# Four-tap convolution on GpSimd, eleven selection rounds before the recurrence, and a new order of recurrence and attention

## Chip, core and metric

One NeuronCore of a Trainium2 chip runs the whole program in one launch. The metric is the device time of that launch in microseconds (us). The core has five engines with queues of their own: TensorE (PE in the profile, PEld its weight loads), VectorE (DVE), ScalarE (ACT), GpSimd (POOL) and SyncE (SP), which here only issues DMAs. An engine works through its queue in order and waits on counting semaphores.

## What is computed

The reference is one inference step of a small decoder: 512 prompt tokens and 8 sequences with 4 new tokens each (32 sample tokens, 544 columns in all), two layers, width 1024, float32. A layer multiplies its input by one wide matrix, and the columns go to four branches of width 256:

```python
y_a = attn(q, k, v, qi, ki, wi)            # a token indexer scores all keys; only the top 128 (129) count
y_b, rwkv_state, shift_buf = rwkv7_mix(cols[..., B_START:B_END], ...)   # linear recurrence, 64x64 states
y_c, convc_buf = gated_short_conv(cols[..., C_START:C_END], ...)        # three-tap convolution, gated
y_d, convd_buf, lru_h = rglru_block(cols[..., D_START:D_END], ...)      # four-tap convolution, gated recurrence
mix = concatenate([y_a, y_b, y_c, y_d]) @ w_out                         # then layer norm, 16 experts, layer norm
```

The four-tap convolution of branch D adds to `w[0]*x[t-3]` the products of three more taps and a bias, per channel. Its result feeds two sigmoid gates (matrix products) and the input of that branch's recurrence. The selection of branch A needs, per query, a threshold below the largest 128 (prompt) or 129 (sample) scores.

## The kernel before

All matrices are float32 and every layer is written as five queue programs that run side by side: `sync_program`, `pool_program`, `tensor_program`, `scalar_program` and `vector_program`. The order inside each queue is written out by hand. Semaphores count events per layer (`nth(l, name, n)`). Inside the recurrence, three lists of names (`RW_PE`, `RW_DVE`, `RW_ACT`, lines 175 to 182) say which count on `rw_mm`, `rw_v` and `rw_a` stands for which result, so the lists must follow the order in the queues.

A layer goes through these stages.

*Projections.* `columns` of TensorE computes 17 chunks of 128 channels by 544 tokens (line 755), ScalarE copies each from PSUM to a ring of four buffers `fm` (line 1391), and the small products of the branches stand between the chunks: indexer, LoRA, key norms, bonuses, and after chunk 11 the gate products `lru_gates` (lines 815 and 816, by `product`). Chunks 0 to 6 belong to the recurrence, 7 and 9 to the four-tap convolution, 8 and 10 to its output gate, 11 to 16 to the three-tap convolution in two halves.

*VectorE during the projections* (`columns` of `vector_program`): it mixes the chunks, computes decays (`decays`), key rates (`key_rates`, `bonus`), both halves of the four-tap convolution (`conv_d`, lines 1952 to 1965, by `taps`, lines 1892 and 1895), normalised keys (`key_norms`, lines 1940 to 1948: clamp, reciprocal of 1152 columns, products), the inputs of the recurrence (`chunk_inputs`, lines 2053 to 2059) and branch D (`lru_decay`, `lru_input`, `lru`, lines 1969 to 2000). In between it runs ten rounds of the selection. A round finds the eight largest values of each of four score tiles (512, 384, 256 and 544 columns; line 2300) and replaces them by a very small number (line 2307).

*GpSimd during the projections* (`pool_program`): row stores, then `conv_c` for both halves (lines 588 to 616), each when its three chunks are there. ScalarE may copy chunks 15 and 16 only when `conv_c` is through with the first half's buffers (`fc_used`).

*Recurrence* (`rwkv`): the prompt is cut into 8 blocks of 64 tokens. TensorE forms many 64x64 products (`diagonal`, line 893), VectorE masks and adds from PSUM (lines 2073, 2104, 2148, 2164), ScalarE copies (line 1391). At the start TensorE computes `bar0 ab0 bar1 ab1 kar0`, after a wait for all 17 chunk copies; VectorE's masks follow in `first(0)`, `first(1)`, `keys(0)`. In between VectorE runs selection rounds 10 to 15 in quarters (`selection_quarter`, lines 2317 and 2319): 24 quarters, six of them in the last part. That last part passes the state through the blocks: `step(c)` on TensorE, `state(c)` on VectorE, by turns. Beside it run the sample tokens: products with their old states (`s_m0`, `s_m1`), two masked reductions (lines 2183 and 2187), `spread` (lines 2194 to 2197), three products for each half of the new states (`s_t0`, `s_t1`) and their scaling (line 2210). `finish_selection` (round 16, then the additive masks `bias`, lines 2325 to 2330) stands before that scaling. The end of the recurrence, `rw_v` at its last count, lets SyncE load key pages (line 484) and GpSimd value pages (line 651).

*Attention* (`prompt_attention`, `sample_logits`, `sample_attention`): for each of four blocks of 128 queries logits (line 1120), masking and row maxima on VectorE (`masked`, lines 2352 to 2359), exponentials on ScalarE (`exps`, line 1637), scaling (`normed`, line 2367), transposes and products with the values (`output(i)`, lines 1139 and 1128). Before, all of `masked(0..2)` precede `normed(0..2)`; TensorE does `output(0)`, `logits(3)`, `output(1)`, both halves of the sample logits (line 1177), `output(2)`, `output(3)`. Norms of branch B stand between (`y_sums`, line 1099).

Then come the output projection, the norm, the router and the experts, which the diff leaves alone.

## Time and profile before

| | us |
|---|---|
| median of three runs | 1319.84 |
| lowest and highest | 1317.95, 1325.25 |
| the profiled execution's own time | 1318.73 |
| span of its trace | 1317.1 |
| mean granted clock of TensorE over the span | 0.927 of full |

The profile shows one execution. Its page lists busy time per engine, the chain of work that ended last (each piece led back to what released it) and groups of instructions by source line. A line such as 893 belongs to a helper that many products share, so times within a stage are read from the timeline (instructions in order of time) and from windows (busy time of each engine in a stretch). A float32 matrix product shows as two instructions. Idle time before an instruction stands in brackets, with the engine whose work ended it.

### The profile page before, as it was taken

Reading aid. Unit: us, or ns where it says so; the run is one execution under the profiler, and the core shown is the slowest. Engines: PE = TensorE matmul, PEld = TensorE weight load, DVE = VectorE, ACT = ScalarE, POOL = GpSimd, SP = SyncE. Lnnn points to the kernel's source line nnn. Section 1 sums busy time; section 2 is a strip of 40 time slices with the busy share of each in tenths; the row PEclk is TensorE's granted clock in tenths of the full one; section 3 lists DMA queues with packets and bytes.
Section 4 is the critical chain, followed back from the end, with each engine's and each line's share of the span. In section 5 each row is a group of like instructions: output and inputs, shape, how many; then the busy total and the mean of one; then the engine's idle time right before and its main releaser. Section 6 shows DMA issues by size and latency. Waiting matters only on the chain.

```text
span 1317.1 us, 24577 instructions
## 1 busy us (share of the span) xinstructions
PE 1127.5 (86%) x9786; PEld 685.4 (52%) x9786; DVE 651.4 (49%) x1353; ACT 327.9 (25%) x774; POOL 165.4 (13%) x225
## 2 busy tenths in 40 slices
PE   8999998987899369999599999999778982999940
PEld 4587777973545323332256777889434451333310
DVE  0046898875633611111643588988772453111128
ACT  0234341303421111111244343412053210111100
POOL 0130008105000020000301000450230002000020
PEclk9989999998999679999799999999889985999975
DMA  7199110007660769997522112100296247699742
GB/s 285 56 395 354 48 56 26 7 3 225 208 260 1 319 233 354 423 423 257 203 77 65 57 48 64 33 21 4 64 275 256 101 168 300 245 410 421 300 150 103
DMA packets 66548, 240.37 MB, mean 183 GB/s; under 512 B 8738, under 2 KB 28354, under 8 KB 57026
## 3 DMA queue, kind: packets, MB, share of 16 engines
q1 hardware_dynamic: 46800, 169.15, 33.9%
q0 software_dynamic: 14592, 52.10, 10.9%
q10 hardware_dynamic: 5042, 17.54, 3.3%
q8 instruction: 79, 1.29, 0.4%
q14 instruction: 35, 0.29, 0.1%
HBM read 190.21 MB, written 50.78 MB: 183 GB/s over the span
## 4 chain that ended last, share of the span: by engine, by line
PE 82%; DVE 5%; issue 3%; ACT 3%; DMA 2%; SPq 2%; DVEq 2%; POOL 1%; POOLq 0%; ACTq 0%
PE ps L755 20%; PE ps L1299 13%; PE ps L893 11%; PE ps L1256 8%; PE ps L1314 7%; PE ps L701 4%; PE ps L735 4%; SPq L484 2%; PE ps L815 2%; PE ps L1286 2%; PE ps L1128 1%; PE ps L711 1%; ACT arena L1391 1%; PE ps L1235 1%; PE ps L1223 1%
## 5 line engine op out<-in xcount | busy, mean ns | idle before, releaser
L1391 ACT ACTIVATE arena<-ps 128x512 f32<-128x512 f32 (+14 forms) x342 | 142.3, 454 | 612.4 <-PE ps L755 137.3
L755 PE MATMUL ps<-arena 128*128 128x272 f32 x1088 | 259.7, 397 | 0.0
L755 PEld LDWEIGHTS ps<-arena 128*128 128x128 f32 x1088 | 206.4, 192 | 47.8 <-issue 4.0
L1299 PE MATMUL ps<-arena 128*32 128x512 f32 x1536 | 169.7, 592 | 4.8 <-ACT arena L1391 4.8
L893 PE MATMUL ps<-arena 64*64 64x64 f32 (+3 forms) x4016 | 150.6, 234 | 18.8 <-DVE arena L2164 12.1
L893 PEld LDWEIGHTS ps<-arena 64*64 64x64 f32 x4016 | 137.3, 136 | 31.2 <-issue 18.0
L1256 PE MATMUL ps<-arena 128*128 128x512 f32 x256 | 112.4, 594 | 0.0
L1299 PEld LDWEIGHTS ps<-arena 128*32 128x32 f32 x1536 | 51.3, 110 | 116.9 <-issue 116.9
L1314 PE MATMUL ps<-arena 128*32 128x512 f32 x768 | 87.4, 595 | 3.3 <-DVE arena L2623 2.0
L2617 DVE COPY arena<-ps 128x256 f32<-128x256 f32 x24 | 10.2, 425 | 140.2 <-PE ps L1331 140.2
L1256 PEld LDWEIGHTS ps<-arena 128*128 128x128 f32 x256 | 47.5, 189 | 56.5 <-issue 56.5
L711 PE MATMUL ps<-arena 128*128 128x512 f32 x34 | 23.2, 852 | 49.2 <-DMA rows_in<-arena,ints 37.0
L2623 DVE COPY arena<-ps 128x512 f32<-128x512 f32 x24 | 16.6, 693 | 91.0 <-PE ps L1314 91.0
L701 PE MATMUL ps<-arena 128*128 128x420 f32 (+1 forms) x128 | 52.3, 571 | 5.1 <-DMA arena<-in_xT 5.1
L735 PE MATMUL ps<-arena 128*128 128x512 f32 (+1 forms) x128 | 52.7, 569 | 3.1 <-ACT arena L1696 3.1
L1696 ACT ACTIVATE arena<-ps,arena 128x128 f32<-128x128 f32 (+1 forms) x112 | 38.8, 451 | 58.4 <-PE ps L1223 43.4
L1314 PEld LDWEIGHTS ps<-arena 128*32 128x32 f32 x768 | 23.2, 109 | 50.1 <-issue 47.7
L2307 DVE MATCH_REPLACE8 arena<-arena 32x544 f32<-32x544 f32 (+3 forms) x82 | 47.1, 585 | 0.0
L2300 DVE MAX8 arena<-arena 32x8 f32<-32x544 f32 (+3 forms) x82 | 43.7, 589 | 1.7
L1725 ACT ACTIVATE arena<-ps 128x256 f32<-128x256 f32 x24 | 9.3, 386 | 137.6 <-PE ps L1299 137.6
L701 PEld LDWEIGHTS ps<-arena 128*128 128x128 f32 x128 | 24.9, 196 | 31.8 <-issue 26.7
L711 PEld LDWEIGHTS ps<-arena 128*128 128x128 f32 x34 | 9.2, 281 | 61.9 <-DMA rows_in<-arena,ints 37.3
(348 smaller groups left out, 1333.2 us busy)
## 6 DMA issues: line engine op xcount, KB each, us to landing
arena<-in_w_gu SPq DMA_DIRECT2D x32, 2048.0 KB, 13.8
arena<-in_w_dn SPq DMA_DIRECT2D x32, 1024.0 KB, 14.4
arena<-in_wf SPq DMA_DIRECT2D x34, 512.0 KB, 3.7
rows_in<-arena POOLq DMA_DIRECT2D x12, 1024.0 KB, 25.1
arena<-rows_in SPq DMA_DIRECT2D x24, 512.0 KB, 13.8
rows_out<-arena ACTq DMA_DIRECT2D x24, 512.0 KB, 8.6
arena<-in_cache_v POOLq DMA_DIRECT2D x64, 128.0 KB, 5.7
arena<-in_cache_k SPq DMA_DIRECT2D x64, 128.0 KB, 5.5
```

Of the source, the lines that this page charges most:

```text
L701: mm = pe.matmul(ps[:, k, 0:w], m.xT[:, c, row_tile(k % NT)], m.wa[:, c, a:a + w], start=c == 0, stop=c == KC - 1, skip_group_check=True)
L711: pe.matmul(ps[:, 7, :], ident, m.consts[:, 0:512], start=True, stop=True)
L735: mm = pe.matmul(ps[:, k % 2, 0:w], m.xT[:, c, row_tile(i)], m.wa[:, c, a:a + w], start=c == 0, stop=c == KC - 1)
L755: mm = pe.matmul(ps[:, 2 + 2 * h + n % 2, 0:HALF], m.wf[n % 3][:, c, :], m.xT[:, c, h * HALF:h * HALF + HALF], start=c == 0, stop=c == KC - 1)
L893: mm = pe.matmul(out[q], lhsT[q], rhs[q], start=start, stop=stop, skip_group_check=check)
L1256: mm = pe.matmul(ps[:, 2 * (i % 2) + h, :], m.yT[:, c, row_tile(i)], m.wout[c // 4][:, c % 4, 512 * h:512 * h + 512], start=c == 0, stop=c ...
L1299: mm = pe.matmul(ps[q, 3 + k, :], m.xgT[:, c, q], m.w_gu[HOME[i]][:, c, :], start=c == 0, stop=c == KC - 1, skip_group_check=True)
L1314: mm = pe.matmul(ps[q, 5 + h, :], m.hT[:, f, q], m.w_dn[HOME[i]][:, f, 512 * h:512 * h + 512], start=f == 0, stop=f == 1, skip_group_check ...
L1391: return act.activation(out, in_, ACT.Copy)
L1696: ins = act.activation(m.xT[:, c, P * i:P * i + n], ps[:, 4 + c // 4, n * (c % 4):n * (c % 4) + n], ACT.Identity, bias=m.lnc[:, 1, c:c + 1 ...
L2300: dve.max(m.top8[c][rows], m.score[c][rows])
L2307: dve.match_replace(m.score[c][rows], m.top8[c][rows], m.score[c][rows], TAKEN)
```

## The change

- `conv_d` moves from VectorE's program to GpSimd's, ahead of `conv_c`. There a tap is a multiplication into a scratch tile and an addition, with drains between. It waits for its chunk and for the indexer's last tiles (`relu_done`, `rl_used`), whose memory its output takes. ScalarE's copies of chunks 11 to 14 now wait for `conv_done`, which GpSimd raises after each half, in place of VectorE's `fm_used`.
- VectorE runs one selection round more before `lru`, so the recurrence holds rounds 11 to 15: 20 quarters, two of them in the last part.
- The recurrence starts with `bar0 kar0`, and the wait for the last chunk copies stands behind them. VectorE's masks follow that order. In its last part the sample tokens' products are spread between the steps, and `finish_selection` leaves it.
- `finish_selection` now follows `masked(0)` in attention. `logits(3)` precedes `output(0)`, `masked(3)` precedes `normed(2)`, and the two halves of the sample logits stand before and behind `output(2)`, on ScalarE as on TensorE.
- The key pages lie in memory as (sequence, page, half, key), so a page's two halves are adjacent for each partition: pieces of 1024 bytes instead of 512. The sample logits read them with a stride.

The core of the diff:

```diff
-RW_PE = counts("bar0 ab0 bar1 ab1 kar0 d2_0 d2t_0 d2_1 d2t_1 kar1 d4_0 d4t_0 d4_1 d4t_1 tb0 tb1 d8_0 d8_1 tv0 tv1 "
+RW_PE = counts("bar0 kar0 ab0 bar1 ab1 d2_0 d2t_0 d2_1 d2t_1 kar1 d4_0 d4t_0 d4_1 d4t_1 tb0 tb1 d8_0 d8_1 tv0 tv1 "
                "x4_0 x4_1 ta0 ta1 x2_0 x2_1 tk0 tk1 x1_0 x1_1 wv0 wv1 xt_0 xt_1 s_bar ft_0 ft_1 s_t s_kar "
-               "z1_0 z1_1 s_d2 z2_0 z2_1 s_z s_wv z3_0 z3_1 s_pp pp0 pp1 gx0 gx1 h0 y0 h1 y1 "
-               "h_1 s_rc h_2 h_3 s_m0 s_m1 h_4 h_5 h_6 s_y h_7 y_7 s_t0 s_t1")
-RW_DVE = counts("q0 dt0 q1 dt1 km0 d2_0 d2_1 km1 d4_0 d4_1 x8_0 x8_1 x4_0 x4_1 x2_0 x2_1 x1_0 x1_1 s_q s_km z1_0 z1_1 s_x "
-                "z2_0 z2_1 s_z z3_0 z3_1 s_pp pp0 pp1 gx0 gx1 t1 t2 s_rc t3 t4 t5 s_w t6 s_u0 t7 s_u1 t8 s_t0 s_t1")
+               "z1_0 z1_1 s_d2 z2_0 z2_1 s_z s_wv z3_0 z3_1 s_pp pp0 pp1 gx0 gx1 h0 y0 s_rc h1 s_m0 s_m1 y1 "
+               "h_1 h_2 h_3 s_y h_4 h_5 s_t0 h_6 s_t1 h_7 y_7")
+RW_DVE = counts("q0 km0 dt0 q1 dt1 d2_0 d2_1 km1 d4_0 d4_1 x8_0 x8_1 x4_0 x4_1 x2_0 x2_1 x1_0 x1_1 s_q s_km z1_0 z1_1 s_x "
+                "z2_0 z2_1 s_z z3_0 z3_1 s_pp pp0 pp1 gx0 gx1 t1 s_rc s_w t2 t3 t4 t5 s_u0 t6 s_u1 t7 s_t0 t8 s_t1")
...
-    m.K = [view(at, 2, 4, PAST) for at in (R2, XT0)]
+    m.K = [view(at, 4, NPAGE, 2, PAGE) for at in (R2, XT0)]
...
-            sp.dma_start(m.K[g][:, :, j:j + 1, PAGE * c:PAGE * c + PAGE],
-                         din["cache_k"][bass.ds(l * NPHYS + page, 1)].rearrange("z p q k -> p q z k"))\
+            sp.dma_start(m.K[g][:, j, c:c + 1, :, :],
+                         din["cache_k"][bass.ds(l * NPHYS + page, 1)].rearrange("z p q k -> p z q k"))\
...
-    def taps(out, tmp, src, w):
+    def taps(out, tmp, src, w, bias=None):
 
         width = SEQ if len(src.shape) == 2 else DS
+        first = 4 - len(w)
 
         def at(k):
-            return src[:, 1 + k:1 + k + width] if len(src.shape) == 2 else src[:, :, 1 + k:1 + k + width]
-
-        pool.tensor_scalar(out, at(0), w[0], None, mul)
-        for k in range(1, 3):
+            return src[:, first + k:first + k + width] if len(src.shape) == 2 else src[:, :, first + k:first + k + width]
+
+        pool.tensor_scalar(out, at(0), w[0], bias, mul, add) if bias is not None else pool.tensor_scalar(out, at(0), w[0], None, mul)
+        for k in range(1, len(w)):
             pool.tensor_scalar(tmp, at(k), w[k], None, mul)
             pool.drain()
             pool.tensor_tensor(out, out, tmp, add)
             pool.drain()
+
+    def conv_d(l, j):
+        convd = m.param("convd").rearrange("p (j b t) -> p j b t", j=2, b=DB)
+        tail = m.small("convd").rearrange("p (j c) -> p j c", j=2)
+        dw, db = m.param("dw"), m.param("db")
+        n = 7 + 2 * j
+        xb = n % 4
+        pool.wait_ge(s["fm_copied"], nth(l, "fm_copied", n + 1))
+        pool.wait_ge(s["relu_done"], nth(l, "relu_done", 12))
+        pool.wait_ge(s["rl_used"], nth(l, "rl_used", 12))
+        pool.tensor_tensor(m.turn, m.const("ones"), m.const("ones"), ALU.add)
+        pool.drain()
+        pool.tensor_copy(m.fm_s[xb][:, :, 0:3], convd[:, j, :, :])
+        pool.drain()
+        w = [dw[:, 4 * j + k:4 * j + k + 1] for k in range(4)]
+        taps(m.xc[:, j, 0:SEQ], m.tap[:, 0:SEQ], m.fm_p[xb], w, db[:, j:j + 1])
+        taps(seqs(m.xc[:, j, SEQ:T]), seqs(m.tap[:, SEQ:T]), m.fm_s[xb], w, db[:, j:j + 1])
+        pool.tensor_copy(tail[:, j, 0:3], m.fm_p[xb][:, SEQ:3 + SEQ])
+        pool.tensor_copy(tail[:, j, 3:27].rearrange("p (b t) -> p b t", t=3), m.fm_s[xb][:, :, 4:7])
+        pool.drain().then_inc(s["conv_done"], 1)
 
...
+        conv_d(l, 0)
+        conv_d(l, 1)
...
-        pe.wait_ge(s["fm_copied"], nth(l, "fm_copied", NCH))
         pe.wait_ge(s["job_out"], nth(l, "job_out", 12))
-        for g in range(2):
-            wide(2 * g, lambda k: cut(m.BE, g, k), lambda k: both(g, k)).then_inc(s["rw_mm"], 1)
+        def barred(g):
+            return wide(2 * g, lambda k: cut(m.BE, g, k), lambda k: both(g, k))
+
+        def turned_bar(g):
             for k in range(8):
                 mm = diagonal(ps[:, 4 + g, CH * k:CH * k + CH], cut(AE, g, k), cut(m.BE, g, k))
-            mm.then_inc(s["rw_mm"], 1)
+            return mm
+
+        barred(0).then_inc(s["rw_mm"], 1)
         wide(6, lambda k: cut(m.KE, 0, k), lambda k: both(0, k)).then_inc(s["rw_mm"], 1)
+        pe.wait_ge(s["fm_copied"], nth(l, "fm_copied", NCH))
+        turned_bar(0).then_inc(s["rw_mm"], 1)
+        barred(1).then_inc(s["rw_mm"], 1)
+        turned_bar(1).then_inc(s["rw_mm"], 1)
...
+        grown(0).then_inc(s["rw_mm"], 1)
+        read(0).then_inc(s["rw_mm"], 1)
+        v("gx0")
+        for p in range(2):
+            mm = diagonal(ps[:, 4, NS * p:NS * p + NS], m.sPP[:, p, 1, :], m.sQ[:, p, 1, 0:NS])
+        mm.then_inc(s["rw_mm"], 1)
+        grown(1).then_inc(s["rw_mm"], 1)
+        v("gx1")
+        v("s_rc")
+        pe.wait_ge(s["state_in"], nth(l, "state_in", 32))
+        for p in range(2):
+            diagonal(ps[:, 5 + p, :], m.sLR[:, p, :], m.TB[:, p]).then_inc(s["rw_mm"], 1)
+        read(1).then_inc(s["rw_mm"], 1)
+        step(1)
+        step(2)
+        step(3)
+        v("s_w")
+        sample_rows_out().then_inc(s["rw_mm"], 1)
+        step(4)
+        step(5)
+        v("s_u0")
+        sample_state(0).then_inc(s["rw_mm"], 1)
+        step(6)
+        v("s_u1")
+        sample_state(1).then_inc(s["rw_mm"], 1)
+        step(7).then_inc(s["rw_mm"], 1)
 
...
         logits(2)
+        logits(3)
         pe.wait_ge(s["yn_std"], nth(l, "yn_std", 1))
         output(0)
-        logits(3)
         output(1)
-        sample_logits(l)
+        sample_logits(l, 0)
         output(2)
+        sample_logits(l, 1)
         output(3)
 
-    def sample_logits(l):
...
+            elif n >= 11:
+                act.wait_ge(s["conv_done"], nth(l, "conv_done", 1 if n < 13 else 2))
...
-        for g in range(2):
-            act.wait_ge(s["s_lg_mm"], nth(l, "s_lg_mm", g + 1))
-            copy(m.s_lg[g][:, 0:PAST], ps[:, 2 - 2 * g, :])
-            copy(m.s_lg[g][:, PAST:T], ps[:, 3 - 2 * g, 0:NS]).then_inc(s["s_lg"], 1)
+        sample_logits(0)
         turned(2)
         output(2)
+        sample_logits(1)
...
-        conv_d(l, 0)
         block_queries(l)
         select_rounds(1)
-        conv_d(l, 1)
...
-        select_rounds(1)
+        select_rounds(2)
...
-        quarters = iter(range(4 * 10, 4 * 16))
+        quarters = iter(range(4 * 11, 4 * 16))
...
-        first(0)
-        first(1)
+        near(0)
         keys(0)
+        turned(0)
+        near(1)
+        turned(1)
...
         mm("h0")
         state(0)
-        select(4)
-        mm("h_1")
-        state(1)
+        select(1)
         mm("s_rc")
         tt(m.sLR[:, :, NS:2 * NS], ps[:, 4, 0:2 * NS].rearrange("p (k n) -> p k n", n=NS), m.AR[:, 1, :, SEQ:T], add)\
             .then_inc(s["rw_v"], 1)
-        mm("h_2")
-        state(2)
-        mm("h_3")
-        state(3)
-        mm("h_4")
-        state(4)
+        select(1)
         for p in range(2):
             mm(f"s_m{p}")
             tt(m.sM[p], ps[:, 5 + p, :].rearrange("p (b n) -> p b n", n=CH),
...
-        mm("h_5")
-        state(5)
+        for c in range(1, 4):
+            mm(f"h_{c}")
+            state(c)
 
         def spread(p):
             own = m.const("s_rows").unsqueeze(2).broadcast_to([P, DB, CH])
-            tt(m.sW[:, p, :], m.sW[:, p, :], m.sPP[:, p, 0, :], add)
-            dve.drain()
             tt(m.UEb[p], m.sW[:, p, :].unsqueeze(1).broadcast_to([P, DB, CH]), own, mul)
             tt(m.VEb[p], m.sT[:, 2, p, :].unsqueeze(1).broadcast_to([P, DB, CH]), own, mul).then_inc(s["rw_v"], 1)
 
-        select(2)
-        mm("s_y")
-        spread(0)
-        mm("h_6")
-        state(6)
-        spread(1)
-        mm("h_7")
-        state(7)
-        finish_selection()
-        for p in range(2):
+        def sample_out(p):
             mm(f"s_t{p}")
             tt(m.TB[:, p], ps[:, 4 + p, :].rearrange("p (b n) -> p b n", n=CH),
                m.ec_s[:, p].unsqueeze(2).broadcast_to([P, DB, CH]), mul).then_inc(s["rw_v"], 1)
+
+        mm("s_y")
+        tt(m.sW, m.sW, m.sPP[:, :, 0, :], add)
+        mm("h_4")
+        state(4)
+        dve.drain()
+        spread(0)
+        mm("h_5")
+        state(5)
+        spread(1)
+        mm("h_6")
+        state(6)
+        sample_out(0)
+        mm("h_7")
+        state(7)
+        sample_out(1)
+        dve.drain()
 
     def y_centred(l):
         dve.wait_ge(s["fc_used"], nth(l, "fc_used", 2))
...
         y_centred(l)
-        for i in range(3):
-            masked(i)
-        for i in range(3):
-            normed(i)
+        masked(0)
+        finish_selection()
+        masked(1)
+        masked(2)
+        normed(0)
+        normed(1)
         masked(3)
+        normed(2)
...
```

The bodies that are only moved are left out: VectorE's old `conv_d`, the old order of the recurrence's end on TensorE (`grown` and `read` for both groups first, then the steps, then both sample state products) and `sample_logits`, which now takes the half `g` as an argument.

## Rows read from the trace of the kernel before

**Rows 1.** The page's first part: busy us, share, instructions of TensorE.

```profile
PE 1127.5 (86%) x9786; PEld 685.4 (52%) x9786; DVE 651.4 (49%) x1353; ACT 327.9 (25%) x774; POOL 165.4 (13%) x225
```

**Rows 2.** Chain of waits, 170 to 232 us: start, length, what.

```profile
217.47 3.55 issue
```

**Rows 3.** Timeline: end of the projections, first masks in both layers.

```profile
219.52 1.40 ACT L1391 ACTIVATE arena<-ps 128x272 f32<-128x272 f32 x6 [10.10 <-POOL arena L616]
...
224.65 6.56 DVE L2073 TENSOR_TENSOR arena<-ps,arena 128x512 f32<-128x512 f32 x12 [3.67 <-PE ps L893]
...
866.24 6.56 DVE L2073 TENSOR_TENSOR arena<-ps,arena 128x512 f32<-128x512 f32 x12 [2.14 <-PE ps L893]
```

**Rows 4.** Windows: us; PE, PEld, DVE, ACT, POOL busy; clock; DMA share; GB/s.

```profile
181.00:217.50 36.50, 36.47 (x159) 29.70 (x157) 34.81 (x82) 12.37 (x21) 16.94 (x17) 1.00 0.10 30
...
262.00:284.60 22.60, 22.44 (x653) 22.25 (x648) 17.00 (x41) 1.48 (x3) 0.00 (x0) 1.00 0.01 4
288.30:291.20 2.90, 0.01 (x2) 0.00 (x0) 2.70 (x4) 0.00 (x0) 0.00 (x0) 1.00 0.00 0
292.70:299.00 6.30, 3.60 (x24) 1.74 (x26) 5.90 (x16) 0.78 (x2) 0.00 (x0) 0.50 0.01 1
326.00:330.00 4.00, 4.00 (x11) 1.47 (x10) 0.47 (x1) 0.19 (x1) 0.00 (x0) 0.50 1.13 311
```

**Rows 5.** Chain of waits, 270 to 334 us: recurrence's end, attention.

```profile
291.29 2.36 DVE arena L2319 x5
...
295.40 7.73 PE ps L893 x40
...
325.77 3.71 PE ps L1120 x8
```

**Rows 6.** Timeline of TensorE in layer 1: second half of the sample logits.

```profile
979.24 0.18 PEld L1177 LDWEIGHTS ps<-arena 128*32 128x32 f32 x8 [0.20 <-DMA arena<-in_cache_k]
```

**Rows 7.** Timeline, 136 to 182 us: chunk 7, key norms, gate products, chunk inputs.

```profile
136.48 0.75 ACT L1391 ACTIVATE arena<-ps 128x272 f32<-128x272 f32 x3 [6.67 <-PE ps L755]
...
158.12 1.32 ACT L1525 ACTIVATE arena<-ps 128x512 f32<-128x512 f32 x4
...
161.14 0.76 DVE L1940 TENSOR_SCALAR arena<-arena 128x1152 f32<-128x1152 f32 x1
...
174.93 1.02 PE L815 MATMUL ps<-arena 128*128 128x512 f32 x2
...
177.46 1.36 DVE L2057 TENSOR_TENSOR arena<-arena 128x1152 f32<-128x1152 f32 x1
```

**Rows 8.** GpSimd's groups by shape: count, busy us, mean ns, idle before.

```profile
L592 POOL TENSOR_TENSOR arena<-arena 128x512 f32<-128x512 f32 x8 | 10.2, 1272 | 1.2 <-issue 0.2
...
L588 POOL TENSOR_SCALAR arena<-arena 128x512 f32<-128x512 f32 x4 | 6.3, 1567 | 0.7 <-issue 0.7
```

**Rows 9.** Timeline, 182 to 216 us: GpSimd's first convolution beside VectorE.

```profile
184.08 2.09 DVE L2300 MAX8 arena<-arena 128x8 f32<-128x512 f32 x4
...
198.65 0.19 POOL L604 COPY arena<-arena 128x16 f32<-128x16 f32 x1 [2.23 <-issue]
...
207.29 3.53 POOL L590 TENSOR_SCALAR arena<-arena 128x512 f32<-128x512 f32 x1 [0.17 <-issue]
208.19 1.28 DVE L1978 SCALAR_TENSOR_TENSOR arena<-arena 128x1088 f32<-128x1088 f32 x1
...
213.26 0.25 POOL L592 TENSOR_TENSOR arena<-arena 128x32 f32<-128x32 f32 x1
...
214.20 1.35 POOL L592 TENSOR_TENSOR arena<-arena 128x32 f32<-128x32 f32 x1
```

**Rows 10.** Timeline of VectorE, 262 to 304 us: state 0, end of the selection.

```profile
277.58 0.29 DVE L2164 TENSOR_TENSOR arena<-ps,arena 128x128 f32<-128x128 f32 x1 [0.45 <-PE ps L893]
...
296.97 0.70 DVE L2300 MAX8 arena<-arena 32x8 f32<-32x544 f32 x1
...
300.68 0.17 DVE L2330 TENSOR_TENSOR arena<-arena 32x32 f32<-32x32 f32 x1
```

More of the change, by code:

```diff
@@ new lines, in sample_logits @@
+        pe.wait_ge((s["k0_in"], s["k1_in"])[g], nth(l, f"k{g}_in", 256))
+        a = 2 - 2 * g
+        pe.wait_ge(s["qb_ready"], nth(l, "qb_ready", 1))
+        pe.wait_ge(s["lg_taken"], nth(l, "lg_taken", 4))
+        for j in range(4):
+            for p in range(2):
+                pe.matmul(ps[32 * j:32 * j + 32, a, :].rearrange("m (c k) -> m c k", c=NPAGE), m.QB[:, p, 4 * g + j, :], m.K[g][:, j, :, p, :],
+                          start=p == 0, stop=False, skip_group_check=True)
+        pe.matmul(ps[:, a, :], spread[0:NS, P * g:P * g + P], bias[0:NS, 0:PAST], start=False, stop=True,
+                  skip_group_check=True)
@@ L2083, in select, with near @@
                 selection_quarter(*divmod(next(quarters), 4))
-        def first(g):
+        def near(g):
             mm(f"bar{g}")
@@ L2091, in first, with turned @@
             ins.then_inc(s["rw_v"], 1)
+        def turned(g):
             mm(f"ab{g}")
```

71 lines of the change are left out of this document (21 added, 50 removed).

## The prediction

> **What bounds the kernel now.** First the page: TensorE is busy 86% of the span [rows 1], so a gain has to shorten a stretch in which TensorE waits or runs slowly. The change touches three such stretches of each of the two layers: the end of the projections, the recurrence's last third, and attention. Experts, output projection and norms keep their code and are taken to move along unchanged.
>
> *End of the projections.* The chain of waits shows TensorE standing still 3.55 us between the last projection and the recurrence [rows 2]. The timeline tells why: ScalarE copies the last two chunks only after GpSimd's first convolution, a wait of 10.10 us [rows 3]. VectorE has little to spare there: it is busy 34.81 of 36.5 us [rows 4] and idles 3.67 us (layer 0) and 2.14 us (layer 1) before the recurrence's first mask, from 220.98 and 864.10 on [rows 3]. Who is late next when TensorE stops waiting is therefore VectorE.
>
> *Recurrence.* From 262 to 284.6 TensorE is busy 22.44 of 22.6 us [rows 4]; nothing that VectorE gives back there counts. Behind 284.6 it waits for VectorE twice: 2.9 us without work (288.3 to 291.2), then 2.7 idle us before the sample products at 295.40; these run partly at a granted clock of 0.50, 1.2 GHz [rows 4, 5].
>
> *Attention.* The fourth block's logits lie on the chain, 3.71 us, at a clock of 0.50 [rows 4, 5]. Key loads matter once: in layer 1 the second half of the sample logits starts 0.20 us after a key page lands [rows 6].
>
> **The change, part by part** (us per layer).
>
> *Convolution on GpSimd.* VectorE loses both conv_d, but gains little of their length. key_norms starts at 161.14 because conv_d(1) precedes it; without that it waits for ScalarE's square root, which ends at 159.44 [rows 7]. So 1.7 us come free; conv_d(0)'s share falls into an earlier wait for ScalarE's head copies.
>
> GpSimd needs per conv_d four multiplications (1.57) and three additions (1.27) of 512 columns [rows 8], the same seven of 32 columns (some 0.3 each; a free addition takes 0.25 [rows 9]), small copies and gaps of some 0.15: 6.3 + 3.8 + 2.2 + 2.7 = 15. The first multiplication also adds a bias, which no row shows; I take 1.57, with 3.53, the longest multiplication seen [rows 9], as the upper end; below the one-operation row there is no reason to go. The first instruction after a long pause is followed by a 2.23 us gap [rows 9]. Chunk 7 is copied at 137.2 [rows 7]: the first convolution ends at 137.2 + 2.2 + 15 + some 3.5 of blocking (next paragraph) = 158, the second would end at 173, ahead of the gate products at 174.93 [rows 7].
>
> But the two engines exclude each other. GpSimd's multiplication of 207.29 took 3.53 us, because VectorE's two-input operations ran until 209.47; a 32-column addition took 1.35 instead of 0.25 beside another one [rows 9]. After the reciprocal key_norms and chunk_inputs are seven two-input operations of some 1.35 (they end at 177.46 + 1.36 [rows 7]). They meet GpSimd's last addition and its seven small operations, so both take turns. I place GpSimd's end at 182 and VectorE's delay at c = 3.0 (bounds 0, never meeting, and 6, four full GpSimd operations in their way). TensorE waits in the second gate product from 176.1 to 182: 5.9 us. A pause of that length can halve the clock, as before the sample products [rows 4], some 1.6 us more.
>
> In row 207.29 GpSimd lost the turn to an operation (208.19) that asked later. The Trainium skill ("SBUF — State Buffer", Who interferes with whom) says that whoever issues first gets the port pair for the whole instruction. By that rule GpSimd would get every second turn, and c would be 3.6 instead of 3.0, 1.2 us more in all; row 207.29 contradicts it, so I keep 3.0. The same section has VectorE's one-input tensor_scalar block GpSimd too; no row here shows it, and by it key_norms' first operation would wait up to one GpSimd operation more.
>
> *Eleventh round.* Four maxima (2.09 [rows 9]) and four replacements (2.36 [rows 5]) with their gaps: 4.6 us, on VectorE's tight stretch. VectorE reaches the masks at 220.98 - 1.7 + 4.6 + 3.0 = 226.9 in layer 0, at 864.10 + 5.9 = 870.0 in layer 1.
>
> *Recurrence entry.* TensorE now starts bar0 and kar0 before waiting for the last chunk copies, so the 3.55 us wait is covered by those two groups. With the gate stall it starts at 217.5 + 5.9 = 223.4; its first result is used 2.1 us later (VectorE's idle time in layer 1 [rows 3]), 225.5, or 227 with the 3.6 of layer 0 (221.02 to 224.65 [rows 2, 3]). VectorE's 226.9 decides. Against 224.65 and 866.24 [rows 3] the masks start 2.3 and 3.8 later. **Entry: +6.1 in both layers together**, bounds 0 (c = 0) and +12 (c = 6).
>
> VectorE's key masks now precede the DT mask, which puts TensorE's first wait 1.3 us later behind the masks' start; slack of TensorE covers that (five groups of products lie before it), and if not it costs 1.3.
>
> *Recurrence tail.* Four quarter rounds, the final round and the bias building leave it. State 0 is at 277.58 [rows 10]; the same three groups of products follow, 2 us each, now with 1.9 us of sample products between them: step 1 at 285.3. VectorE's two reductions hold state 1 to 286.1. Three states at 0.85 a turn and the sample rows: 288.7. State 4 and the first spread (two operations of 0.69): 290.7. Sample state products 2.6 (six passes of 0.43), step 6, the second 2.6, step 7 and two VectorE operations: 297.7, where it was 303.85. **-6 per layer, -12.** Seen from the other side: the two waits (2.9 + 2.7) and 2.1 of half clock go [rows 4], 1.7 of new turns come. If the clock falls again it is -4; at best -6.5.
>
> *Attention.* The final selection round and the biases, 296.97 to 300.85, 3.9 us [rows 10], were hidden by the sample products of 295.40 (7.73 us [rows 5]). Now they stand between masked(0) and masked(1): masked(2) ends 4.8 later, the third exponentials 1.6 later, and with them ScalarE's first turned copy. But logits(3) fills that pause, and its 3.71 leave the way to output(1), which thus starts 2.1 earlier. Splitting the sample logits around output(2) keeps their sum; the exponentials behind the second half take back 0.9. With output(0) no longer at clock 0.50, 0.5 more: **-1.7 per layer, -3.4** (bounds +1.6, nothing filled, and -2.5).
>
> *Key pages.* SP's queue issues as many loads in the same order, each with half the packets. In layer 1 the last lands at 979.2, 33.6 us after the recurrence; the second half of the sample logits will ask at 36.8. Margin 3.2: no cost, no gain. GpSimd's queue has the value loads behind its convolutions as before, far behind. conv_c waits behind conv_d, but its inputs come at 196, after 182. ScalarE's copies of chunks 11 to 14 wait for conv_d instead of VectorE; chunk 13 leaves TensorE after the gate stall anyway.
>
> **Sum.** +6.1 - 12 - 3.4 = -9.3 against the profiled execution, 1318.73 (span 1317.1): 1309.4. The median is 1.1 above it, so 1310.
>
> **Rivals.**
> *GpSimd is on time* (0.2): the operations hardly meet, c is 0, conv_d(1) ends before 176, entry 0. For it: maxima, replacements and the reciprocal do not meet GpSimd's work in any row. Then -15.4: 1304.
> *The gain stays off the path* (0.18): the clock falls in the tail (-8), attention gives 3.2 instead of taking, entry +6: about +1, 1321. For it: VectorE works 5.90 of 6.3 us in the tail and TensorE still idles between its turns [rows 4].
> *GpSimd comes too late* (0.12, slower): conv_d(1) holds TensorE in the gate products. If every operation of conv_d is blocked (3.53 for a multiplication, 1.27 + 1.3 for an addition, 1.35 for a small one [rows 9]), each convolution takes 34 us and the second ends at 207; TensorE stalls 31, starts at 248.5, and the masks come 26 late in each layer: +52 - 15.4 = +37, 1355. It makes the kernel slower by over 0.5% once the entry costs 22 in all, which is a second convolution that ends after 192. Against it: the mean addition and first multiplication are at their unblocked length [rows 8].
>
> **How the numbers follow.** The forecast itself has 0.5, range 1302 to 1316: entry bounds against tail -8. No change means within 0.5% (6.6 us, about what a measurement of this kernel can tell): 1313.2 to 1326.4. Faster: 0.42 of the forecast's 0.5 plus 0.2 = 0.62; same: 0.08 + 0.18 = 0.26; slower 0.12. The range takes in all but the late GpSimd and some edges: 1300 to 1326.
>
> **What would show it.** Right: GpSimd's second four-tap convolution ends near 182 and TensorE waits some 6 us between the first and second gate product; masks start near 227 at VectorE's hand; no wait over 1 us for VectorE among the recurrence's last products; fourth logits before the first transposes. Wrong: a gate stall over 16 us, masks that start before 224, a tail longer than 24 us behind state 0, or second sample logits waiting for pages.

## The result and the profile after

| | before | after |
|---|---|---|
| median, us (6 runs each, same chip) | 1324.31 | 1311.57 |
| lowest and highest | 1317.95, 1325.25 | 1308.91, 1316.64 |
| profiled execution's own time | 1318.73 | 1311.37 |
| span of its trace | 1317.1 | 1309.7 |

The ratio is 0.9916, with a 95% interval of 0.9888 to 0.9945: the changed kernel is faster by 0.8%, and the 1310 that was predicted is 1.6 us off. As a change it is 2.9 off: the medians fell by 12.7, and the forecast was 9.8 below the 1319.84 that it started from. One execution of what follows, of run 10's kernel, took 2053 us at a granted clock of 0.55 and is left out of its times.

The table below gives the stages of the two traces, counted from the start of TensorE's first gate product (174.93 and 818.42 before, 174.17 and 813.48 after). All later comparisons use these columns, because the clock of the stages ahead differs from run to run.

| us | first mask | state 0 | attention starts | output projection | last part (state 0 to attention) | attention |
|---|---|---|---|---|---|---|
| before, layer 0 | 49.72 | 102.65 | 129.07 | 189.08 | 26.42 | 60.01 |
| before, layer 1 | 47.82 | 100.76 | 127.23 | 187.42 | 26.47 | 60.19 |
| after, layer 0 | 49.75 | 102.76 | 123.04 | 181.98 | 20.28 | 58.94 |
| after, layer 1 | 49.41 | 101.73 | 122.02 | 182.92 | 20.29 | 60.90 |

Up to state 0 the change costs 0.11 and 0.97 us, the recurrence's last part gives 6.14 and 6.18, attention gives 1.07 and takes 0.71: 11.6 us in all. The two profiled executions differ by 7.4 only; the other 4.2 lie outside these stages (0.8 won ahead of layer 0's first gate product, 2.9 lost between the layers, 2.0 lost behind layer 1's attention). Part of that is the clock: one group of layer 1's projections took 9.32 us at a granted clock of 0.82, where it took 7.64 at 1.00 before.

**Gate products** (where [rows 7] had 174.93 for the first). TensorE's timeline after, layer 0 and then layer 1, in which line 838 is the gate product:

```profile
174.17 1.02 PE L838 MATMUL ps<-arena 128*128 128x512 f32 x2
...
178.35 2.08 PE L838 MATMUL ps<-arena 128*128 128x512 f32 x2 [3.01 <-POOLq L614]
...
180.51 2.05 PE L838 MATMUL ps<-arena 128*128 128x512 f32 x2
...
817.76 1.12 PE L838 MATMUL ps<-arena 128*128 128x512 f32 x2 [3.12 <-POOLq L614]
```

Line 614 raises `conv_done`: the second convolution is 3 us late in both layers. The windows of layer 0 show what follows (columns as in [rows 4]; the one before the DMA share is the granted clock):

```profile
174.00:178.00 4.00, 1.34 (x6) 0.70 (x4) 3.81 (x7) 2.90 (x6) 3.40 (x5) 1.00 0.40 131
178.00:182.00 4.00, 3.65 (x6) 1.94 (x7) 3.85 (x12) 0.87 (x2) 0.25 (x2) 0.50 0.00 0
185.00:189.00 4.00, 4.00 (x18) 3.27 (x18) 3.85 (x11) 1.96 (x3) 0.00 (x0) 1.00 0.00 0
```

Behind the wait the products run at 0.50 (1.2 GHz) and take 2.08 instead of 1.02 us. In layer 1 a wait of 3.12 us is followed by the full clock (1.12).

**GpSimd beside VectorE** ([rows 8, 9] before). Four lines of GpSimd's timeline in layer 0, three of VectorE's at the same moments, then one of GpSimd's and one of VectorE's from layer 1:

```profile
139.39 1.11 POOL L589 TENSOR_SCALAR arena<-arena 128x512 f32<-128x512 f32 x1 [0.21 <-issue]
...
156.84 0.76 POOL L589 TENSOR_SCALAR arena<-arena 128x512 f32<-128x512 f32 x1 [0.18 <-issue]
...
168.85 2.58 POOL L591 TENSOR_SCALAR arena<-arena 128x32 f32<-128x32 f32 x1
...
177.02 0.37 POOL L591 TENSOR_SCALAR arena<-arena 128x32 f32<-128x32 f32 x1 [0.17 <-issue]
...
158.72 1.04 DVE L1982 TENSOR_SCALAR arena<-arena 128x1152 f32<-128x1152 f32 x1 [2.88 <-ACT arena L1564]
...
168.71 1.37 DVE L1988 SCALAR_TENSOR_TENSOR arena<-arena 128x1152 f32<-128x1152 f32 x1
170.00 1.28 DVE L1990 TENSOR_TENSOR arena<-arena 128x1088 f32<-128x1088 f32 x1
...
843.63 1.49 POOL L593 TENSOR_TENSOR arena<-arena 128x512 f32<-128x512 f32 x1
843.91 2.37 DVE L2005 SCALAR_TENSOR_TENSOR arena<-arena 128x1088 f32<-128x1088 f32 x1
```

GpSimd's multiplication of 32 columns takes 2.58 us beside VectorE's two-input operations and 0.37 free of them. VectorE's seven operations of `key_norms` and `chunk_inputs` keep their 1.28 to 1.41 us in layer 0: in this stretch GpSimd alone pays. Elsewhere VectorE pays too: the last line, an operation of branch D, takes 2.37 us behind an addition of 512 columns that GpSimd started just ahead of it, and the same operation takes 1.28 in layer 0, where GpSimd was busy with a multiplication. The first operation of `key_norms` starts 15.45 us ahead of the first gate product, where it was 13.79.

**Entry** (against the masks of [rows 3] and state 0 of [rows 10]). VectorE's timeline, layer 0 and layer 1:

```profile
223.92 3.74 DVE L2098 TENSOR_TENSOR arena<-ps,arena 128x512 f32<-128x512 f32 x7 [2.28 <-PE ps L916]
...
276.93 0.29 DVE L2193 TENSOR_TENSOR arena<-ps,arena 128x128 f32<-128x128 f32 x1 [0.45 <-PE ps L916]
...
862.89 6.20 DVE L2098 TENSOR_TENSOR arena<-ps,arena 128x512 f32<-128x512 f32 x12 [0.26 <-PE ps L916]
```

In layer 0 VectorE idles 2.28 us before its first mask, so TensorE decides; in layer 1 it idles 0.26, no more than where it waits for nothing (run 1 below), so VectorE decides.

**Last part of the recurrence** (against the waits and the 7.73 us of [rows 4, 5]). TensorE's timeline after:

```profile
285.82 0.68 PE L916 MATMUL ps<-arena 64*64 64x64 f32 x16 [0.92 <-DVE arena L2193]
286.66 1.85 PE L916 MATMUL ps<-arena 64*64 64x64 f32 x56 [0.16 <-DVE arena L2193]
288.67 0.68 PE L916 MATMUL ps<-arena 64*64 64x64 f32 x16 [0.16 <-DVE arena L2193]
290.06 6.30 PE L916 MATMUL ps<-arena 64*64 64x512 f32 x56 [0.71 <-DVE arena L2218]
297.21 1.10 PE L1136 MATMUL ps<-arena 128*128 128x512 f32 x2 [0.85 <-DVE arena L2222]
```

```profile
290.00:297.20 7.20, 6.30 (x56) 2.70 (x57) 3.19 (x8) 0.60 (x1) 0.00 (x0) 1.00 0.01 2
```

No wait is over 0.92 us (0.93 in layer 1), and the sample products run without a pause and at the full clock, where [rows 4] have 0.50.

**Attention** (against line 1120 in [rows 5]). TensorE's timeline, then a window with the columns as above:

```profile
309.10 1.56 PE L1157 MATMUL ps<-arena 64*128 64x384 f32 x8 [2.45 <-DVE arena L2381]
312.52 1.99 PE L1157 MATMUL ps<-arena 64*128 64x512 f32 x8 [1.86 <-DVE arena L2385]
...
317.07 0.43 PE L1165 MATMUL ps<-arena 128*64 128x128 f32 x2 [1.34 <-ACT arena L1428]
```

```profile
320.00:324.00 4.00, 3.95 (x16) 2.33 (x14) 3.93 (x4) 1.25 (x4) 0.00 (x0) 0.50 1.07 343
```

The fourth block's logits (second line) now run at the full clock, but wait 1.86 us for the third masking, which reads the same PSUM banks. Behind that run of waits the half clock has moved on to the second half of `output(0)` and to `output(1)`.

### The profile page after: what moved, and what is told of

It is laid out like the page before. It is cut to its first block, busy times and chain, and to the rows that moved or that the text cites. A ratio compares the mean times of both kernels' runs of the same rounds, so it can differ in the third digit from the quotient of the medians.

```text
span 1309.7 us, 24635 instructions
## 1 busy us (share of the span) xinstructions
PE 1129.9 (86%) x9786; PEld 686.6 (52%) x9786; DVE 638.1 (49%) x1307; ACT 328.4 (25%) x774; POOL 224.3 (17%) x297
## 4 chain that ended last, share of the span: by engine, by line
PE 73%; DVE 7%; issue 6%; POOLq 4%; ACT 3%; DMA 2%; POOL 2%; DVEq 2%; ACTq 0%; SPq 0%
PE ps L778 13%; PE ps L1336 13%; PE ps L916 10%; PE ps L1293 9%; PE ps L1351 7%; PE ps L724 4%; PE ps L758 4%; POOLq L592 2%; PE ps L1165 2%; POOLq L594 2%; PE ps L1323 2%; ACT arena L1428 1%; PE ps L734 1%; POOL arena L591 1%; POOL rows_in L684 1%
## 5 line engine op out<-in xcount | busy, mean ns | idle before, releaser
L778 PEld LDWEIGHTS ps<-arena 128*128 128x128 f32 x1088 | 206.5, 191 | 48.2 <-issue 4.0
L916 PE MATMUL ps<-arena 64*64 64x64 f32 (+3 forms) x4016 | 145.6, 231 | 5.5 <-DVE arena L2193 2.5
L916 PEld LDWEIGHTS ps<-arena 64*64 64x64 f32 x4016 | 134.6, 134 | 16.8 <-issue 10.0
L1293 PEld LDWEIGHTS ps<-arena 128*128 128x128 f32 x256 | 48.1, 191 | 57.7 <-issue 57.6
L591 POOL TENSOR_SCALAR arena<-arena 128x512 f32<-128x512 f32 (+1 forms) x40 | 50.9, 1273 | 4.1 <-issue 4.1
L2336 DVE MATCH_REPLACE8 arena<-arena 32x544 f32<-32x544 f32 (+3 forms) x90 | 51.6, 585 | 0.0
L2329 DVE MAX8 arena<-arena 32x8 f32<-32x544 f32 (+3 forms) x90 | 47.9, 589 | 1.9
```

Source lines behind the costliest of these rows:

```text
L591: pool.tensor_scalar(tmp, at(k), w[k], None, mul)
L778: mm = pe.matmul(ps[:, 2 + 2 * h + n % 2, 0:HALF], m.wf[n % 3][:, c, :], m.xT[:, c, h * HALF:h * HALF + HALF], start=c == 0, stop=c == KC - 1)
L916: mm = pe.matmul(out[q], lhsT[q], rhs[q], start=start, stop=stop, skip_group_check=check)
L1293: mm = pe.matmul(ps[:, 2 * (i % 2) + h, :], m.yT[:, c, row_tile(i)], m.wout[c // 4][:, c % 4, 512 * h:512 * h + 512], start=c == 0, stop=c ...
L2329: dve.max(m.top8[c][rows], m.score[c][rows])
L2336: dve.match_replace(m.score[c][rows], m.top8[c][rows], m.score[c][rows], TAKEN)
```

## The experiments

Ten runs. The diffs are against the changed kernel, except where noted, and leave out lines that only follow from those shown (counts, indices, moved bodies, the matching order on ScalarE). The times are counted from the first gate product again, and each ratio is to the kernel before on the same chip.

**1. The convolution back on VectorE, all else as changed.**

```diff
@@ pool_program
-        conv_d(l, 0)
-        conv_d(l, 1)
         conv_c(l, 0)
@@ vector_program, columns
+        conv_d(l, 0)
         block_queries(l)
         select_rounds(1)
+        conv_d(l, 1)
         key_norms(l)
```

> The changed kernel with one part undone: the four-tap convolution is back on VectorE, eleven rounds and all new orders stay. Times are counted from the start of TensorE's first gate product; in the changed kernel the first mask of the recurrence comes at 49.75 (layer 0) and 49.41 (layer 1), the last projections start at 10.77 and 7.84. Theory A (the move frees VectorE by 1.7 us only, and costs TensorE a gate stall): the last projections start at 5.6 in both layers again; VectorE reaches the masks 1.7 to 2 later than now, so they come at 49.4 to 50 in layer 0 and at 51 in layer 1, and the whole kernel stays within 3 us of the changed one, ratio to the kernel before 0.990 to 0.995. Theory B (the move is what pays for the eleventh round): VectorE gets back the 4.3 and 5.6 us that the two convolutions took on it, the masks come 8 to 10 later in each layer, and the ratio is 1.004 or more.

Ratio 0.9966 (0.9937 to 0.9995), between the two theories: some 6 us slower than the changed kernel, with intervals that touch. The last projections start at 5.44 again (10.60 and 7.67 in the changed kernel), and the masks come at 51.62 and 51.40, by 1.9 and 2.0 later. State 0 comes 3.3 and 3.9 later (106.10 and 105.66). Timeline of layer 0 (the mask, then TensorE's wait for it), then a window:

```profile
225.33 6.20 DVE L2111 TENSOR_TENSOR arena<-ps,arena 128x512 f32<-128x512 f32 x12 [0.26 <-issue]
...
229.13 11.07 PE L914 MATMUL ps<-arena 64*64 64x64 f32 x250 [5.62 <-DVE arena L2111]
```

```profile
230.00:234.00 4.00, 4.00 (x82) 4.00 (x80) 3.28 (x7) 0.60 (x1) 2.87 (x8) 0.50 0.02 4
```

TensorE stands still 5.62 us and then runs at 0.50. The masks are near theory A in layer 1 (it gave 51), and later than its 49.4 to 50 in layer 0: VectorE is ready for them 3.9 us later than in the changed kernel (51.36 against 47.47), and 2.0 later in layer 1. Only 1.3 and 1.2 of that lie ahead of branch D. Most of the other 2.6 and 0.8 lies in it, where GpSimd's three-tap convolution now runs beside VectorE's two-input operations (one of 1088 columns takes 2.37 us in both layers). The half clock behind a late VectorE (1.5 us in layer 0, 1.9 in layer 1) was in neither theory.

**2. Ten rounds; four quarters more in the last part.**

```diff
@@ vector_program, columns
-        select_rounds(2)
+        select_rounds(1)
         lru(l)
@@ vector_program, rwkv
         state(0)
-        select(1)
+        select(4)
         mm("s_rc")
...
-        select(1)
+        select(2)
```

> The changed kernel with ten selection rounds before the recurrence instead of eleven; the four quarters that this leaves over go back into the recurrence's last part (four behind state 0, two behind the sample rows). In the changed kernel that part, from state 0 to the first product of attention, takes 20.3 us in both layers. Theory A (VectorE's selection work made the last part long): it grows by 3 us per layer (four quarters are 4.6, some 1.6 of idle time is there to take them); the masks stay where they are in layer 0, where VectorE idles 2.28 before them, and come 2.6 earlier in layer 1; in sum +3 to +4, ratio 0.993 to 0.995. Theory B (the new order of the last part made it short, the quarters fit into VectorE's idle time there): the last part grows by 1 us at most, and layer 1's earlier masks make the kernel 1 to 2 us faster than the changed one, ratio 0.990.

Ratio 0.9939 (0.9902 to 0.9976). The last part took 22.56 and 23.77 us, 2.3 and 3.5 more; the masks came at 49.81 and 46.84. Theory A to the letter, so at these places quarters cost. Whether it was they that made the last part of before long is the next question's.

**3. The kernel before, VectorE relieved, old order kept** (diff against the kernel before).

```diff
@@ vector_program, columns
-        select_rounds(1)
+        select_rounds(2)
         lru(l)
@@ vector_program, rwkv
         state(0)
-        select(4)
+        select(1)
...
-        select(2)
+        select(1)
         mm("s_y")
...
-        finish_selection()
@@ vector_program, attention
         masked(0)
+        finish_selection()
         masked(1)
```

> The kernel before with only VectorE's selection work moved: eleven rounds before the recurrence, one quarter in place of four behind state 0, one in place of two behind state 5, the end of the selection in attention between the first and the second masking. The order of the products in the recurrence's last part, the convolution on VectorE, the entry and the key layout are those of before. The last part took 26.4 us before and takes 20.3 in the changed kernel. Theory A (the selection work made it long): 21.5 or less. Theory B (the order of the sample products made it long): 23.5 or more. In between both have a share. The entry is later than before by up to 4.6 us (the eleventh round) less the 3.67 and 2.14 that VectorE idled there.

The last part took 26.91 and 26.19 us: nothing won (1330.16 us in a single run). Timeline of layer 0, then a window:

```profile
283.12 0.29 DVE L2164 TENSOR_TENSOR arena<-ps,arena 128x128 f32<-128x128 f32 x1 [4.17 <-PE ps L893]
...
290.95 2.35 PE L893 MATMUL ps<-arena 64*64 64x64 f32 x40 [2.93 <-DVE arena L2164]
...
295.19 8.12 PE L893 MATMUL ps<-arena 64*64 64x64 f32 x40 [1.90 <-DVE arena L2164]
```

```profile
293.00:297.00 4.00, 2.10 (x28) 1.35 (x26) 3.35 (x8) 0.82 (x2) 0.00 (x0) 0.50 0.01 2
```

VectorE idles 4.17 us at the start, and TensorE's wait of 2.93 (two reductions stand between states 3 and 4) is there as in [rows 4]. The wait before the sample products is 1.90 instead of 2.78 us, but the half clock takes that back: here it sets in earlier (the products of 290.95 take 2.35 us, and 1.38 in the kernel before). With the order of before, less selection makes the part no shorter: theory B.

**4. The end of the selection in VectorE's two waits of the last part.**

```diff
@@ vector_program, rwkv
+        selection_round(16)
         mm("h_6")
         state(6)
         sample_out(0)
+        biases()
         mm("h_7")
@@ vector_program, attention
         masked(0)
-        finish_selection()
```

> The changed kernel with the end of the selection back in the recurrence, but cut in two: the last round (1.7 us) stands before state 6, the additive masks (2.1 us) before state 7, where VectorE waits 1.73 and 2.15 us for TensorE. Theory A (in attention the end of the selection stands on the chain: TensorE waits 2.45 to 2.73 us for the second masking and 1.86 for the third): the last part of the recurrence stays at 20.3 us (up to 0.5 more), attention gets 2 to 3 us shorter per layer than the 58.94 and 60.90 of the changed kernel, ratio 0.986 to 0.989. Theory B (as the prediction had it, the fourth block's logits fill that pause, and TensorE's own work bounds attention): attention gets at most 0.7 shorter per layer, and the kernel stays within 1.5 us of the changed one.

Ratio 0.9891 (0.9855 to 0.9926), not to be told from the changed kernel's. The last part stayed at 20.28 and 20.30, as both theories allow. In attention the second half of the sample logits came 34.77 and 35.49 us after the start, instead of 37.12 and 37.52: theory A's chain is there, worth 2.0 to 2.4. But from there to the output projection it took 24.4 us instead of 21.8 and 23.4. TensorE's timeline in `output(3)` of layer 0, and the window around it:

```profile
338.91 1.97 PE L1165 MATMUL ps<-arena 128*64 128x128 f32 x8 [1.87 <-ACT arena L1428]
```

```profile
338.00:342.00 4.00, 3.09 (x13) 2.43 (x14) 3.77 (x5) 1.39 (x5) 0.00 (x0) 0.50 0.81 334
```

A wait of 1.86 or 1.87 us for ScalarE stands there in every run with this order of attention; behind it the clock fell here. Attention as a whole: 59.22 and 59.91, nearer theory B's size, for another reason.

**5. Gate products split around chunk 12.**

```diff
@@ tensor_program, projections
-        lru_gates(l)
-        columns(l, 12, 13, 14, 15, 16)
+        lru_gates(l, 0)
+        columns(l, 12)
+        lru_gates(l, 1)
+        columns(l, 13, 14, 15, 16)
```

> The changed kernel with TensorE's and ScalarE's order changed: both gate products of the first half, then chunk 12, then both of the second half, so that the second convolution has some 8 us more. Theory A (behind the gate stall VectorE is next: it idles only 2.28 us before the masks in layer 0 and 0.26 in layer 1): the stall of 3.0 us and the half clock behind it go, the end of the projections comes 4 to 6 us earlier in layer 0 and 2 to 3 in layer 1, but the first mask only 2.0 to 2.3 earlier in layer 0 and within 0.5 of now in layer 1: 2 to 3 us in all, ratio 0.989 to 0.991. Theory B (TensorE bounds the entry in both layers): the masks come earlier by as much as the projections end earlier, 6 to 8 us in all, ratio 0.986. Should VectorE's branch D wait for the later sigmoids, the masks come 1 to 2 later instead.

Ratio 0.9926 (0.9896 to 0.9956): nothing gained. The stall is gone, and projections run through at the full clock; the recurrence's first product starts 41.3 us behind the gate product instead of 47.6 in layer 0. The masks come at 48.88 and 48.97 only, and state 0 at 103.33 and 103.41, later than in the changed kernel. Timeline of layer 0, then a window:

```profile
220.10 6.20 DVE L2101 TENSOR_TENSOR arena<-ps,arena 128x512 f32<-128x512 f32 x12 [0.26 <-PE ps L917]
...
223.90 16.29 PE L917 MATMUL ps<-arena 64*64 64x64 f32 x430 [4.07 <-DVE arena L2101]
```

```profile
226.00:230.00 4.00, 4.00 (x82) 4.00 (x81) 2.72 (x6) 0.60 (x1) 3.26 (x9) 0.51 0.00 0
```

VectorE is next, as theory A had it. The stall of 3 us had been hiding VectorE's lateness, and TensorE's new wait of 4.07 us brings the half clock in its turn. In layer 0 the mask gained 0.9 and not the 2.0 to 2.3 of theory A: VectorE was ready 1.15 us later than in the changed kernel (line 2024, the scan of branch D, took 3.53 us instead of 2.48, beside GpSimd's second three-tap convolution).

**6. The copies waited for first.**

```diff
+        pe.wait_ge(s["fm_copied"], nth(l, "fm_copied", NCH))
         barred(0).then_inc(s["rw_mm"], 1)
         wide(6, lambda k: cut(m.KE, 0, k), lambda k: both(0, k)).then_inc(s["rw_mm"], 1)
-        pe.wait_ge(s["fm_copied"], nth(l, "fm_copied", NCH))
```

> The changed kernel with TensorE's wait for the last chunk copies put back in front of the recurrence's first two product groups. Theory A (as the prediction had it: the copies are late and the new order hides the wait): TensorE stands still some 3 us before the recurrence, as the 3.55 and 3.19 of before, and the first mask comes 3 us later than the 49.75 of the changed kernel in layer 0. Theory B (GpSimd's three-tap convolution now ends early enough, so the copies are on time and the new order has little left to hide): TensorE waits for the copy of chunk 16 alone, 0.8 to 1.2 us; the first mask comes at 50.5 to 51 in layer 0 and, VectorE being the bound there, unchanged within 0.3 in layer 1.

1310.50 us in a single run. TensorE's timeline of layer 0 has a wait again:

```profile
222.24 5.97 PE L916 MATMUL ps<-arena 64*64 64x128 f32 x120 [0.93 <-ACT arena L1428]
```

It is 0.93 us in either layer, and layer 0's mask comes at 50.58, by 0.83 later. Theory B in layer 0: the new order of the entry hides 0.9 us now. In layer 1 the mask came at 50.66, but there the gate products ran at the half clock, and TensorE decided.

**7. The key pages laid out as before.**

```diff
-    m.K = [view(at, 4, NPAGE, 2, PAGE) for at in (R2, XT0)]
+    m.K = [view(at, 2, 4, PAST) for at in (R2, XT0)]
```

> The changed kernel with the key pages laid out in memory as before (pieces of 512 bytes, twice the packets). In the trace of before the 32 loads of layer 1 keep SyncE's queue 28.19 us, in the changed kernel 21.16. Theory A (as the prediction had it: no cost, no gain): SyncE's queue takes 28 us again, and neither half of the sample logits waits for a page; they start some 28 and 37 us after the recurrence's end as in the changed kernel. Theory B (the new layout is what lets the first half move ahead of the third block's output): one of the halves of layer 1 waits 1 us or more for a key page.

1316.87 us in a single run. SyncE's queue took 26.69 us for layer 1's pages (21.16 with the new layout); TensorE waited for none, and the sample logits started at 28.47 and 37.54 us of attention, as with the new layout (28.45 and 37.52). Theory A; attention took 60.55 and 60.91.

**8. A candidate: the split gates of 5, the ten rounds of 2, and the quarters at the waits of 4.**

```diff
@@ vector_program, rwkv
+        select(2)
         mm("h_6")
         state(6)
         sample_out(0)
+        select(2)
         mm("h_7")
```

> A candidate: the changed kernel with the split gate products, ten rounds before the recurrence, and the four quarters that this leaves over in the recurrence's last part at the two places where VectorE waits for TensorE (two before state 6, two before state 7; waits of 1.73 and 2.15 us, two quarters take 2.2 to 2.6). Theory A (VectorE bounds the entry once the gate stall is gone): the first mask comes 4.6 earlier than the 48.9 of the split gates, at 44.3 to 45 in both layers, the last part takes 21 to 21.6 us, and the kernel is 6 to 8 us faster than the changed one, ratio 0.985 to 0.988. Theory B (quarters in the last part cost what they cost with ten rounds, +2.3 and +3.5, wherever they stand): the last part takes 22.6 or more and the gain over the changed kernel is 2 to 4 us, ratio 0.989 or more.

Ratio 0.9821 (0.9787 to 0.9856), 1302.16 us: it beats both kernels. The masks come at 43.39 in both layers, state 0 at 96.40 and 96.39, the last part takes 20.84 and 20.85: the four quarters cost 0.56 us here instead of 2.3 and 3.5.

```profile
217.20 3.75 DVE L2101 TENSOR_TENSOR arena<-ps,arena 128x512 f32<-128x512 f32 x7 [0.46 <-PE ps L917]
```

On VectorE's timeline of layer 0, it waits 0.46 us for TensorE, which has no wait there at all: the two arrive together. Theory A, and more of it: the gain is 12 us (run 9). Against the split gates state 0 comes 7 us earlier, 5.5 at the masks and 1.4 from the half clock, which no longer follows.

**9. The changed kernel again, beside the candidate.** No edit.

> The changed kernel itself, so that the candidate is compared with it on one chip. Theory A expects it 6 to 8 us slower than the candidate, theory B 2 to 4. Its own ratio to the kernel before should be within 0.9888 to 0.9945 again.

Ratio 0.9923 (0.9896 to 0.9951), 1314.45 us, 12 us above the candidate: more than either theory had.

**10. The candidate with the convolution on VectorE** (the edit of 1 on 8).

> The candidate with ten rounds in the waits, with the four-tap convolution back on VectorE: what the move to GpSimd is worth once nothing else holds the recurrence's entry. In the candidate the first mask comes at 43.39 in both layers, TensorE being just ahead of VectorE. Theory A (the move gives VectorE 3 to 4 us: 1.7 ahead of the reciprocal and the rest from two-input operations of branch D that no longer meet GpSimd's three-tap convolution): the mask comes at 46.7 to 47.2, TensorE stands still and its clock falls behind that, state 0 comes 3.5 to 5 later than the candidate's 96.4; the kernel is 7 to 10 us slower than the candidate, ratio 0.987 to 0.990. Theory B (the 1.7 us of the prediction are all): the mask comes at 45 to 45.5 and the kernel is 3 to 4 us slower, ratio 0.984 to 0.985.

Ratio 0.9863 (0.9771 to 0.9956), 1304.96 us in three executions; the ratio is too wide to tell the theories apart, the stages are not. The masks come at 45.34 and 44.98, 1.95 and 1.6 later than the candidate's, state 0 at 97.66 and 97.78, by 1.3 and 1.4. Theory B: here the move is worth the 1.7 us of the prediction.

## Why the prediction was right or wrong

The total was right, and its largest term. Two terms were too large with opposite signs. (The sum as written, 1309.4 and 1.1, gives 1310.5.)

- *"So 1.7 us come free"*: right. `key_norms` starts 1.66 earlier, and run 10 shows 1.6 to 1.95 at the masks. Run 1 shows more, 3.9 and 2.0, because the move also shifts GpSimd's three-tap convolution against VectorE's branch D, which no term had.
- *GpSimd's ends, 158 and 182*: 154.7 and 178.2, so the gate stall was 3.0 and not 5.9. That the second convolution is held up was right (by some 7.7 us, against 9), and so was the half clock behind the stall in layer 0. Too high was the hold-up of the first, 3.5, where it lost about 1.5 us, and the price of the multiplication that adds a bias: 0.76 and 1.11 us, below the 1.57 of [rows 8]. Not going below "the one-operation row" was a slip of 0.8 us each time.
- *"c = 3.0"*: this step failed. In this stretch VectorE lost 0.3 us (1.04 instead of 0.76 in one operation), the lower bound. The seven operations were to meet "GpSimd's last addition" of 512 columns; it ended at 167.19, and the first of the seven started at 167.27. So they met operations of 32 columns only, five in layer 0. Two of these (168.85 and 172.99) were passed by a later operation of VectorE, as in the 3.53 of [rows 9]; three were not. Part of the small c is thus luck in time: where GpSimd's addition did come first, VectorE paid 1.1 us (843.91).
- By the Trainium skill's "SBUF — State Buffer", Who interferes with whom, GpSimd should have had every second turn and c been 3.6. The trace disagrees: the operation of 168.85 was passed by VectorE's of 170.00.
- *Eleventh round, 4.6*: right. Between the two last operations of branch D that surround it VectorE took 9.3 us for two rounds, and 4.7 for one.
- *"VectorE's 226.9 decides"*: half right. In layer 1 it decides, with the masks 1.59 later than before (forecast 3.8, less the 2.7 of c). In layer 0 TensorE decides: its stall cost 3.0 us and some 3 of half clock, and VectorE was ready at 47.47, where it was at 49.15 in layer 1; its branch D lost 0.6 us to GpSimd in layer 0 and 2.2 in layer 1. Entry: +1.1 at state 0 (+1.6 at the masks) instead of +6.1, within the bounds 0 to +12. One sign of being wrong came with it: layer 0's masks started at 223.92, before 224.
- *"The 3.55 us wait is covered by those two groups"*: the wait went, but not by that. GpSimd's three-tap convolution took 16.4 us (200.63 to 217.05) where it took 23.2 (196.23 to 219.43), so the copies are late by 0.9 only (run 6). It is not the stall that gives them time: without it (run 5) the convolution again ended ahead of the last projection.
- *Recurrence tail, -6 per layer*: right, -6.14 and -6.18. But of the edits summed under it, the order of the products is the one that the gain hangs on: selection work taken out of the old order gives nothing (run 3), and put back into the new one at VectorE's waits, four quarters cost 0.56 (run 8) and the end of the selection nothing (run 4). At the old places four quarters cost 2.3 and 3.5 (run 2); no run has the new order with all the selection work of before.
- *Attention, -1.7 per layer*: this step failed as well, with -1.07 and +0.71. Attention took, in the nine profiles with this order of it, 57.6 to 63.3 us, 60.5 on average over 18 stretches, against 60.0 and 60.2 before. "Logits(3) fills that pause": it waits 1.86 us itself. "With output(0) no longer at clock 0.50": its second half is at 0.50.
- *Key pages, no cost, no gain*: right (run 7).
- The rivals: of "GpSimd is on time" the c of 0 came true, not the punctual convolution; of "the gain stays off the path" only its part on attention did. "GpSimd comes too late" would have needed an end after 192, and it was 178.

The errors of the two failed terms, 5.0 too much cost and 3.0 too much gain, partly cancel: the stages gave 11.6 us where the sum had 9.3. That the time was 1.6 us off is in part luck: the kernel before took 4.5 us more in the result than in the three executions that the prediction started from.

## What to carry to other kernels

Two engines can be late for the same point by nearly the same time: taking the wait of one away then gains nothing (run 5), relieving the other moved layer 0's masks not at all and layer 1's by 2.6 us (run 2), but both together, with the quarters in front of waits, gave 12 us (run 8). Before work is moved between stages, look at where an engine waits inside the stage it shall leave: four quarter rounds cost 0.56 us in front of two waits and 2.3 to 3.5 a few lines earlier. And a term that lumps an order and a load needs a run with each alone before the gain is put down to either.

## What the runs showed of the hardware

- *GpSimd's multiplication with a bias* (two operations in one instruction, 512 columns) took 0.76 and 1.11 us in layer 0 and 0.76 and 1.07 in layer 1, where that with one operation takes 1.57 [rows 8]. On 32 columns both take 0.36 or 0.37.
- *GpSimd beside VectorE*: an addition of 512 columns on GpSimd that comes first costs VectorE's two-input operation 1.1 us (843.91: 2.37 instead of 1.28; before, the operation of 199.91 in the same way). A multiplication of GpSimd waits instead (204.50: 2.84 instead of 1.57, while VectorE's of 204.72 kept 1.28).
- *GpSimd's first instruction after a long pause* is followed by a gap: 2.23 us after 57.39 us of idling (layer 0, chunk 7), as the one of [rows 9], and 1.86 after 61.09 us in layer 1. After 22.38 us of idling, ahead of the three-tap convolution, there was none. Whether the pause makes the gap, or the kind of instruction that ends it, no run tells. The moved convolution thus spared the later one its gap, which no term had.
- *Half clock behind a wait is not the same each time.* Behind the gate stall of 3 us, in the six profiles that have it (after, and runs 2, 4, 6, 7, 9), the products ran at 0.50 in all six layers 0 and in two of six layers 1. Behind the 1.87 us wait of `output(3)` the rest of attention took 21.8 us at the full clock, or 23.4 to 24.5. These 2.6 us are part of the 5.7 over which attention in this order is spread; the rest lies ahead of the second half of the sample logits, which starts at 35.3 to 38.9 us. What decides it stays open.
